# Half-row sums and gate chunks redistributed over a transformer block's mixer, its ring narrowed from six chunks to four, a tenth pair buffer added

## The chip, the core and the metric

The kernel runs on one core of a Trainium2 chip. The metric is the device time of one launch, in microseconds. All data is fp32 and comes from HBM, 556 MB in one launch.

## What is computed

One layer of a hybrid backbone on 256 latent and 256 context tokens of width 2048, cut to its skeleton:

```python
mod = silu(c) @ w_mod + b_mod                  # 6 vectors of 2048: shift, scale, gate (mixer), shift, scale, gate (ffn)
n   = rmsnorm(h, g) * (1 + scale) + shift      # also for the context tokens
z   = n @ w_in                                 # 3584 columns: q 1024, k 256, v 256, gMLP u 512, v 512, conv a 512, g 512
out = concat(window_attention(q, k, v, k_c, v_c, sink), chunk_gmlp(u, v), conformer_conv(a, g)) @ w_out
h   = h + gate_mix * out
m   = rmsnorm(h, g_ffn) * (1 + scale_ffn) + shift_ffn
for e in range(16):                            # top-2 of 16 experts, chosen inside one of 4 groups
    h = h + gate_ffn * combine[:, e] * (silu(m @ w_gate[e]) * (m @ w_up[e])) @ w_down[e]
```

## The kernel before

**Stages.** A schedule written out by hand (`make_schedule`, SCHEDULE) gives the order of TensorE's work. After the modulation vectors and the groups A, G and Q0 of the input projection come the groups KV, Q1, V and U (16 `win` steps each, one for each 128 rows), with single steps of other work between them: `gate` (the gate of the feed-forward, 16 chunks of w_mod), `qT`, `kT`, `convsum`, `convsq`, and three parts for each of eight attention heads (0: scores, 1: transposes of the probabilities, 2: product with V). Then comes the output projection, four groups (`wout`, g) of four chunks; behind the last step of group g VectorE adds the gated residual (L1526 to L1529) and TensorE transposes the sum (`hT`, L766). The router follows, then the jobs: each expert's rows in blocks of up to 96, 16 jobs here. Job 0 is always expert 15, whose loads need no router.

**The ring.** `ring` has eight slots of 1 MB. Six of them (PRE_SLOTS) take the chunks of the mixer in turn, in the order of CHUNK_STEPS (95 chunks; `place`, L378). SyncE waits until TensorE has used the chunk six places earlier (`slot_free`, L425) and issues the next (L438). The other two slots are four half slots of 512 KB.

**Half-row sums.** Three of the six modulation vectors, 6 halves of 1024 columns in all, are computed on VectorE: `sum_rows(n)` (L1303 to L1313) takes the next n of 96 rows, waits for each row's load (`half_in`) and for the sum before (`half_step`), and adds row times silu(c) to an accumulator (L1311). GpSimd loads row m into half slot m % 4 as soon as sum m - 4 is done (`load_rows`, L494 to L498), in order. There are two accumulators; `start_half(i)` (L487 to L492) clears one and loads its bias once TensorE has read the half two before it. TensorE reads half i in a step ("half", i) (L587 for i of 2 and more), which needs the first 16(i+1) sums. Halves 0 and 1 are read behind the scores of heads 4 and 7; halves 2 to 5 behind (`wout`, 0, 3), (1, 3), (2, 2) and (3, 1). VectorE's sums stand at fixed places of its own order: 2 ahead of Q0's norm, 5 and 3 ahead of head 0, then between the two softmax steps of each head and behind it, then 17, 16, 13 and 7 ahead of the four residual adds of the projection.

**Pairs.** A job has 12 loads of 2 MB (four each of gate, up and down weights). `job_pairs` names nine buffers of 2 MB: four are pairs of ring slots, the others lie over tensors of the mixer that are dead by then. `first_pairs` gives job 0's buffers in the order of use, `next_pairs` those of the later jobs, which turn over six buffers. SyncE issues job 0's loads behind the last chunk of the mixer, in an order of its own (L441 to L460), each behind the wait that frees its buffer; the loop of the later jobs stands behind them (L462 to L469) and releases by `last_use`.

**Job 0 on the other engines.** TensorE computes gate and up products (L932 or L937), then `table()` for the later jobs, then the down product (L956 or L962). ScalarE copies the residual into `total` (L1230) once pair 6 has been used, and then copies the transposed hidden rows (L1234), for which the down product waits.

Of the kernel before, what the change touches and what calls it, by code (L numbers as in the profile page):

```python
# [9 lines left out]
ALU = mybir.AluOpType  # L10
# [3 lines left out]
P = 128  # L14
D = 2048
# [37 lines left out]
def make_schedule():  # L53
# [28 lines left out]
    halves = {4: 0, 7: 1}  # L82
    hpos = 0
    for g in range(KV_, 7):
        for c in range(4):
# [50 lines left out]

def constants():
# [22 lines left out]
        "slots_n": one * (np.arange(P) % BASE)[None],  # L160
        "slots_m": one * (np.arange(P) % REST)[None],
        "slots_w": one * (REST + np.arange(P) % BASE)[None],
        "slots_0": one * (BLK + np.arange(P) % REST)[None],
# [11 lines left out]
        "cos": cosd, "sin": sind,  # L175
    }
# [17 lines left out]
CONST_COLS = CONST_AT["cos"][0]  # L194
FIRST_CONSTS = CONST_AT["before"][0]


def build(nc, x, ctx, params, consts, b_half, b_gate, w_mix0, w_mix, w_half, w_gmod, w_in, w_out, w_gate, w_up, w_down, out):
    with ExitStack() as stack:
# [19 lines left out]
        silu_c = sb("silu_c", [P, KT, 32])  # L219
        modcol = sb("modcol", [P, 5, KT, 2])  # L220
# [3 lines left out]
        wr_scaled = sb("wr_scaled", [P, KT, NE])  # L224
# [15 lines left out]

        def k_(name):
            at, n = CONST_AT[name]
            if at >= CONST_COLS:
                return heads[:, at - CONST_COLS:at - CONST_COLS + n]
            return const[:, at:at + n]
# [128 lines left out]
        first_kind = sem("first_kind")  # L374
# [3 lines left out]
        def place(n):  # L378
            return (n - NPRE) % PRE_SLOTS

        def slot(n):
            return ring[:, place(n), :]
# [36 lines left out]
        def _(sp):  # L419
            sp.dma_start(param[:, 0:FIRST_PARAMS], params[:, 0:FIRST_PARAMS]).then_inc(par_in, 16)  # L420
            sp.dma_start(const[:, 0:FIRST_CONSTS], consts[:, 0:FIRST_CONSTS]).then_inc(const_in, 16)
            for t in range(TT):
                sp.dma_start(tokens[:, t, :], x[t * P:(t + 1) * P, :]).then_inc(x_in[t], 16)
            for n, (kind, *at) in enumerate(CHUNK_STEPS):
                sp.wait_ge(slot_free, n + 1)  # L425
# [12 lines left out]
                sp.dma_start(to, src).then_inc(landed[place(n)], 16)  # L438
                if n == NUMBER["win", Q0_, 12]:
                    sp.dma_start(const[:, FIRST_CONSTS:], consts[:, FIRST_CONSTS:CONST_COLS]).then_inc(table_in, 16)  # L440
            weights = (w_gate, w_up, w_down)  # L441
# [1382 lines left out]
```

## Time and profile before

| | us |
|---|---|
| median of 3 runs | 1443.22 (1439.74 to 1447.37) |
| profiled execution, whole | 1449.17 |
| its span | 1447.4 |
| TensorE matmul busy | 1299.3 (90%) |
| VectorE busy | 423.1 (29%) |
| ScalarE busy | 209.1 (14%) |
| DMA read | 556 MB, 386 GB/s over the span |

The profile is of one execution. In its views PE is TensorE's matmuls, PEld its weight loads, DVE VectorE, ACT ScalarE, POOL GpSimd, SP SyncE; `x16` counts instructions, a bracket such as `[4.75 <-DVE big L1529]` is the idle time ahead of an instruction and the line that ended it. q1 is the queue of SyncE's loads, q0 that of GpSimd's (the half rows). The granted clock is TensorE's, as a share of 2.4 GHz. A view by stage has for each stretch its length, then busy us and instruction count of PE, PEld, DVE, ACT and POOL, then the granted clock, the DMA engines' busy share and GB/s.

### The profile page before, as it was taken

What the parts mean: (1) busy time and instruction counts of PE and PEld (TensorE: products, weight loads), DVE (VectorE), ACT (ScalarE), POOL (GpSimd) and SP (SyncE); (2) the same over time, 40 slices, a digit from 0 to 9 for tenths busy, and PEclk for the clock granted to TensorE, in tenths of its full rate; (3) what the DMA queues carried; (4) which work ended last, traced back from release to release, by engine and by line L of the source; (5) the groups of instructions that cost most, each with busy time, mean ns of one, the idle gap of its engine ahead of it and who ended that gap; (6) DMA issues with size and microseconds to landing.
All of it is one profiled execution on the core that took longest, in us unless ns stands there. A gap on an engine that the chain in (4) does not pass through costs nothing.

```text
span 1447.4 us, 20580 instructions
## 1 busy us (share of the span) xinstructions
PE 1299.3 (90%) x8742; PEld 618.0 (43%) x8743; DVE 423.1 (29%) x803; ACT 209.1 (14%) x488; POOL 73.6 (5%) x138
## 2 busy tenths in 40 slices
PE   6899999999989998999999999997887887878857
PEld 4556444545445465433632543442442442333223
DVE  2002885877666340202111201021110111111112
ACT  2002101343001133100200110110110110011001
POOL 0001301121322000000000000000000000000000
PEclk9999999999999899999999999999999999999988
DMA  9999659687998899999999999999999999999996
GB/s 380 409 420 384 252 233 397 217 279 271 346 377 313 334 368 426 427 426 424 427 427 415 418 428 427 411 428 427 429 427 428 427 430 428 429 429 428 427 428 263
DMA packets 57450, 559.56 MB, mean 387 GB/s; under 512 B 6688, under 2 KB 6816, under 8 KB 20768
## 3 DMA queue, kind: packets, MB, share of 16 engines
q1 hardware_dynamic: 42768, 504.35, 83.4%
q0 software_dynamic: 14320, 52.01, 9.9%
q10 hardware_dynamic: 288, 2.10, 0.3%
q8 instruction: 60, 0.98, 0.3%
q14 instruction: 14, 0.11, 0.0%
HBM read 556.34 MB, written 2.10 MB: 386 GB/s over the span
## 4 chain that ended last, share of the span: by engine, by line
PE 52%; DMA 39%; DVE 5%; issue 2%; ACT 1%; DVEq 0%; SPq 0%; ACTq 0%
DMA ring<-w_up_dram 11%; PE ps L932 9%; DMA ring<-w_gate_dram 9%; PE ps L937 8%; PE ps L640 7%; DMA ring<-w_half_dram 6%; PE ps L899 5%; PE ps L956 4%; DMA ring<-w_down_dram 4%; DMA big<-w_up_dram 4%; PE ps L962 3%; DVE once L1311 3%; DMA ring<-w_in_dram 3%; PE ps L634 2%; PE ps L645 2%
## 5 line engine op out<-in xcount | busy, mean ns | idle before, releaser
L1680 DVE TENSOR_TENSOR big<-ps,big 128x1024 f32<-128x1024 f32 x60 | 70.7, 1220 | 306.5 <-PE ps L885 161.0
L937 PE MATMUL ps<-ring,big 128*64 128x512 f32 x560 | 132.9, 608 | 22.1 <-DMA ring<-w_up_dram 10.6
L640 PE MATMUL ps<-ring,big 128*128 128x512 f32 x320 | 148.1, 602 | 2.9 <-DMA ring<-w_in_dram 2.3
L1311 DVE SCALAR_TENSOR_TENSOR once<-ring,silu_c,once 128x1024 f32<-128x1024 f32 x96 | 123.2, 1283 | 62.9 <-DMA ring<-w_half_dram 57.2
L899 PEld LDWEIGHTS ps<-probs,big 128*128 128x128 f32 x1024 | 119.2, 191 | 44.3 <-issue 37.6
L899 PE MATMUL ps<-probs,big 128*128 128x96 f32 x1024 | 129.8, 280 | 1.9 <-DVE probs L1684 1.9
L932 PE MATMUL ps<-ring,early 128*32 128x256 f32 x1408 | 90.4, 406 | 30.8 <-DMA ring<-w_up_dram 18.3
L753 PE MATMUL ps<-ring,big 128*128 128x512 f32 x240 | 109.5, 614 | 0.0
L640 PEld LDWEIGHTS ps<-ring,big 128*128 128x128 f32 x320 | 58.4, 191 | 70.4 <-issue 64.8
L937 PEld LDWEIGHTS ps<-ring,big 128*64 128x64 f32 x560 | 36.2, 137 | 104.6 <-issue 66.9
L962 PE MATMUL ps<-ring,once 128*64 128x512 f32 x336 | 77.5, 598 | 3.4 <-DMA ring<-w_down_dram 3.4
L932 PEld LDWEIGHTS ps<-ring,early 128*32 128x32 f32 x1408 | 44.3, 115 | 76.9 <-DMA ring<-w_up_dram 22.6
L956 PE MATMUL ps<-ring,once 128*32 128x512 f32 x576 | 73.2, 602 | 0.3 <-DMA ring<-w_down_dram 0.3
L753 PEld LDWEIGHTS ps<-ring,big 128*128 128x128 f32 x240 | 46.9, 198 | 56.9 <-issue 56.9
L1216 ACT ACTIVATE big<-ps,modcol,scale_ffn 128x96 f32<-128x96 f32 x112 | 39.1, 429 | 206.1 <-PE ps L899 206.1
L1712 DVE TENSOR_TENSOR once<-ps,early 128x512 f32<-128x512 f32 x12 | 8.3, 692 | 192.3 <-PE ps L956 125.4
L498 POOL DMA_DIRECT2D ring<-w_half_dram x96 | 51.1, 532 | 256.9 <-DVE once L1311 256.9
L1216 ACT ACTIVATE early<-ps,modcol,scale_ffn 128x96 f32<-128x96 f32 x144 | 50.3, 429 | 77.7 <-PE ps L899 77.7
L634 PE MATMUL ps<-big,ring 128*128 128x256 f32 x256 | 58.5, 382 | 1.6 <-DMA ring<-w_in_dram 1.6
L937 PE MATMUL ps<-big 128*64 128x512 f32 x224 | 52.4, 600 | 7.5 <-DMA big<-w_up_dram 5.0
L634 PEld LDWEIGHTS ps<-big,ring 128*128 128x128 f32 x256 | 47.8, 190 | 12.5 <-DMA ring<-w_in_dram 4.7
L932 PE MATMUL ps<-big,early 128*32 128x256 f32 x608 | 40.4, 414 | 13.9 <-DMA big<-w_up_dram 7.9
(320 smaller groups left out, 1094.0 us busy)
## 6 DMA issues: line engine op xcount, KB each, us to landing
ring<-w_down_dram SPq DMA_DIRECT2D x48, 2048.0 KB, 23.4
ring<-w_up_dram SPq DMA_DIRECT2D x46, 2048.0 KB, 23.0
ring<-w_gate_dram SPq DMA_DIRECT2D x33, 2048.0 KB, 22.1
ring<-w_half_dram POOLq DMA_DIRECT2D x96, 512.0 KB, 5.9
big<-w_up_dram SPq DMA_DIRECT2D x18, 2048.0 KB, 22.3
ring<-w_mix_dram SPq DMA_DIRECT2D x32, 1024.0 KB, 11.0
late<-w_down_dram SPq DMA_DIRECT2D x16, 2048.0 KB, 23.7
big<-w_gate_dram SPq DMA_DIRECT2D x15, 2048.0 KB, 25.4
```

What stands on the lines that cost most here:

```text
L498: pool.dma_start(half_slots[:, m % HALF_SLOTS, :], w_half[m]).then_inc(half_in[m % HALF_SLOTS], 16)
L634: mm = pe.matmul(Z[b + q // 2][:, (q % 2) * SEQ:(q % 2 + 1) * SEQ], w[:, q * P:(q + 1) * P], nT[:, k, 0:SEQ], start=(k == 0 and q % 2 == 0 ...
L640: mm = pe.matmul(ps[:, b + t, :], nT[:, k, t * P:(t + 1) * P], w, start=(k == 0), stop=(k == KT - 1))
L753: mm = pe.matmul(ps[:, b + t, :], mixT[:, k, t * P:(t + 1) * P], w[:, i, :], start=(k == 0), stop=(k == KT - 1))
L899: mm = pe.matmul(Yb[:, i, at:at + BLK], tokens[:, t, k * P:(k + 1) * P], one_hot[:, t, :], start=(t == 0), stop=(t == TT - 1))
L932: mm = pe.matmul(out_b[0][BASE * f:BASE * (f + 1), :], rows[0][:, k, :], w[:, kk, f * 256:(f + 1) * 256], start=(k == 0), stop=(k == KT - 1))
L937: mm = pe.matmul(out_b[1][REST * f:REST * (f + 1), :], rows[1][:, k, :], w[:, kk, f * N:(f + 1) * N], start=(k == 0), stop=(k == KT - 1))
L956: mm = pe.matmul(Db[0][BASE * q:BASE * (q + 1), :], hT[0][:, (i % 2) * P + BASE * (i // 2):(i % 2) * P + BASE * (i // 2 + 1)], w[:, q * N: ...
L962: mm = pe.matmul(Db[1][REST * (q // 2):REST * (q // 2 + 1), q % 2, :], hT[1][:, (i % 4) * P + REST * (i // 4):(i % 4) * P + REST * (i // 4 ...
L1216: last = act.activation(to[:, k, :], Yb[:, k // 4, at:at + BLK], ACT.Identity, bias=modcol[:, 3, k, 0:1], scale=scale_ffn[:, k:k + 1])
L1311: stt(total, half_slots[:, m % HALF_SLOTS, :], silu_c[:, m % KT, 0:1], total, ALU.mult, ALU.add) \
L1680: tt(y, Yb[:, 2 * h:2 * h + 2, :].rearrange("p a n -> p (a n)"), y, ALU.add).then_inc(summed, 1)
```

## The change

- **Gate chunks:** two behind each quarter of KV and of Q1, instead of three in KV and two behind the first halves of Q1.
- **Sums:** 4 behind the convolution, 3 behind the key rotation, 4 and 3 around the start of the conv variance (before: 5 and 3 there), so that 16 instead of 10 stand ahead of head 0; 15, 15, 12 and 5 in the projection instead of 17, 16, 13 and 7. The gate's bias add moves behind head 1. Halves 0 and 1 are read behind heads 3 and 6.
- **Ring:** from V's first chunk on (NARROW) the mixer uses four slots instead of six. PLACE, EARLIER and LANDINGS hold each chunk's slot, the chunk that had it before, and the count of landings.
- **Pairs:** a tenth buffer, `extra`. Job 0's first load goes into it, ahead of the chunks of Q1; its sixth goes into ring slots 4 and 5 (pair 3) once all of Q1 is used. Pair 6 waits for 88 sums. `first_pairs` and `next_pairs` follow; the tables of slot numbers are loaded last, into `silu_c`, and GpSimd's descriptor scratch shrinks to 4096 bytes to make room.
- **Table:** `table()` of job 0 stands behind its fifth half load instead of behind its eighth.

```diff
@@ make_schedule
-    halves = {4: 0, 7: 1}
+    halves = {3: 0, 6: 1}
-            if g == KV_:
-                seq += [("gate", 3 * c + i) for i in range(3)]
-            elif g == Q1_ and c < 2:
-                seq += [("gate", 12 + 2 * c + i) for i in range(2)]
+            if g in (KV_, Q1_):
+                seq += [("gate", 2 * c + i + (8 if g == Q1_ else 0)) for i in range(2)]
@@
+NARROW, NARROW_SLOTS = NUMBER["win", V_, 0], 4
+PLACE = [(n - NPRE) % (PRE_SLOTS if n < NARROW else NARROW_SLOTS) for n in range(NPRE)]
+EARLIER = [max((m for m in range(n) if PLACE[m] == PLACE[n]), default=n - PRE_SLOTS) for n in range(NPRE)]
+LANDINGS = [PLACE[:n + 1].count(PLACE[n]) for n in range(NPRE)]
@@ build
+        extra = sb("extra", [P, 2 * CH])
-        wr_scaled = sb("wr_scaled", [P, KT, NE])
+        job_slots = silu_c[:].rearrange("p k n -> p (k n)")
+        wr_scaled = late[:, 0:KT * NE].rearrange("p (k e) -> p k e", k=KT)
-        job_pairs += [nT_all[:, 0:2 * CH], big[:, TT * D:2 * TT * D], once[:]]
+        job_pairs += [nT_all[:, 0:2 * CH], big[:, TT * D:2 * TT * D], once[:], extra[:]]
-        first_pairs = (0, 1, 8, 2, 3, 6, 7, 4, 5, 0, 1, 2)
-        next_pairs = (3, 4, 5, 0, 1, 2, 3, 4, 5, 0, 1, 2)
+        first_pairs = (9, 0, 1, 8, 2, 3, 6, 7, 4, 5, 0, 1)
+        next_pairs = (2, 3, 4, 5, 0, 1, 2, 3, 4, 5, 0, 1)
@@ sync
-                sp.wait_ge(slot_free, n + 1)
+                if n == NARROW + NARROW_SLOTS:
+                    sp.wait_ge(slot_free, used_chunk(NARROW - 1))
+                    sp.dma_start(job_pairs[3], weights[5 // 4][FIRST_EXPERT, 5 % 4]).then_inc(job_landed[3], 16)
+                if n == NUMBER["win", Q1_, 0]:
+                    sp.dma_start(job_pairs[first_pairs[0]], weights[0][FIRST_EXPERT, 0]) \
+                        .then_inc(job_landed[first_pairs[0]], 16)
+                sp.wait_ge(slot_free, used_chunk(EARLIER[n]))
-            for i in (5, 2, 0, 1, 3, 4, 6, 7, 8, 9, 10, 11):
+            for i in (6, 3, 1, 2, 4, 7, 8, 9, 10, 11):
                 if s == 6:
                     sp.wait_ge(slot_free, used(U_))
+                    sp.wait_ge(half_step, HALF_SLOTS + 6 * KT - 8)
-                elif i < 9:
-                    sp.wait_ge(slot_free, used_job(2 * s + 1 - SLOTS))
+                elif i < 10:
+                    sp.wait_ge(slot_free, used_job(2 * s - 1 - NARROW_SLOTS) if s else used_chunk(NARROW - 1))
@@ gpsimd, behind the last half row
+            pool.wait_ge(half_step, HALF_SLOTS + 6 * KT)
+            pool.dma_start(job_slots[:], consts[:, LAST_COLS:ALL_COLS]).then_inc(slots_in, 16)
@@ tensor, experts
-                    if m == 1 and first:
-                        table()
-                    elif m == 1:
+                    if m == 1 and not first:
...
+                        if first and m == 0 and i == 4:
+                            table()
@@ vector
             ts(small[:, 32:33], small[:, 63:64], 1.0, None, ALU.mult).then_inc(conv_done, 1)
+            sum_rows(4)
...
             finish_heads(N)
 
+            sum_rows(3)
             dve.wait_ge(csum_done, 1)
...
-            sum_rows(5)
-            dve.wait_ge(gate_bias_in, 16)
-            dve.wait_ge(slot_free, used_chunk(NUMBER["gate", KT - 1]))
-            tt(modrow[:, 1, :], M, modrow[:, 1, :], ALU.add).then_inc(gate_saved, 1)
+            sum_rows(4)
...
                 if h == 1:
+                    dve.wait_ge(gate_bias_in, 16)
+                    dve.wait_ge(slot_free, used_chunk(NUMBER["gate", KT - 1]))
+                    tt(modrow[:, 1, :], M, modrow[:, 1, :], ALU.add).then_inc(gate_saved, 1)
                     head_norm(2)
...
-                sum_rows((17, 16, 13, 7)[g])
+                sum_rows((15, 15, 12, 5)[g])
@@ kernel
-    nc = bacc.Bacc("TRN2", target_bir_lowering=False, num_devices=1)
+    nc = bacc.Bacc("TRN2", target_bir_lowering=False, num_devices=1, dynamic_dma_scratch_size=4096)
```

## Rows read from the trace of the kernel before

**Rows 1.** The page's slices, DMA busy share in tenths of 40 equal slices.
```profile
DMA  9999659687998899999999999999999999999996
```

**Rows 2.** Busy time by stage; then granted clock, DMA share, GB/s.
```profile
198.00:216.00 18.00, 18.00 (x61) 7.14 (x59) 14.99 (x39) 0.00 (x0) 0.00 (x0) 1.00 0.58 234
216.00:257.00 41.00, 41.00 (x159) 19.14 (x159) 24.59 (x46) 8.12 (x15) 4.23 (x8) 1.00 0.95 383
...
360.00:478.00 118.00, 111.70 (x319) 54.54 (x317) 76.67 (x64) 11.04 (x27) 30.28 (x55) 0.97 0.90 335
...
540.00:968.00 428.00, 412.95 (x3686) 180.37 (x3678) 62.23 (x111) 58.50 (x164) 0.00 (x0) 1.00 1.00 423
968.00:1430.00 462.00, 370.76 (x2720) 162.51 (x2720) 66.95 (x118) 45.45 (x124) 0.00 (x0) 0.96 1.00 427
```

**Rows 3.** TensorE's waits, 540 to 968 us: total us, times, longest.
```profile
PE ps L932 <- DMA ring<-w_gate_dram: 1.0, 1, 1.0
```

**Rows 4.** The job loop's loads (L469) issued 903 to 922 us.
```profile
DMA to landing us min/median/max: 8.6/9.2/10.1
```

**Rows 5.** TensorE's waits, 120 to 540 us.
```profile
PE ps L699 <- DVE probs L1454: 3.1, 3, 2.2
```

**Rows 6.** TensorE in order of time, heads and projection: start us, us, what.
```profile
320.68 3.48 PE L640 MATMUL ps<-ring,big 128*128 128x512 f32 x4
...
359.78 7.03 PE L753 MATMUL ps<-ring,big 128*128 128x512 f32 x16
...
390.77 1.84 PE L587 MATMUL ps<-const,once 128*128 128x1 f32 x16
...
434.46 1.97 PE L766 MATMUL ps<-const,big 128*128 128x128 f32 x8 [4.75 <-DVE big L1529]
...
476.96 2.81 PE L587 MATMUL ps<-const,once 128*128 128x1 f32 x16 [1.55 <-DVE once L1311]
479.63 9.61 PE L753 MATMUL ps<-ring,big 128*128 128x512 f32 x16
```

**Rows 7.** TensorE in order of time, end of KV and head 0.
```profile
216.35 2.78 PE L596 MATMUL ps<-ring,silu_c 128*32 128x512 f32 x24
...
255.47 1.04 PE L699 MATMUL ps<-const,probs 128*128 128x128 f32 x8
```

**Rows 8.** VectorE in order of time, convolution to head 0.
```profile
165.24 47.60 DVE L1412 SCALAR_TENSOR_TENSOR once<-yT,late,once 128x256 f32<-128x256 f32 x120
...
217.51 1.22 DVE L1367 TENSOR_REDUCE ss<-work 128x8 f32<-128x1024 f32 x1 [4.48 <-ACT work L1109]
...
231.62 5.46 DVE L1311 SCALAR_TENSOR_TENSOR once<-ring,silu_c,once 128x1024 f32<-128x1024 f32 x4
...
247.59 1.28 DVE L1311 SCALAR_TENSOR_TENSOR once<-ring,silu_c,once 128x1024 f32<-128x1024 f32 x1 [4.29 <-DMA ring<-w_half_dram]
...
250.51 1.23 DVE L1445 TENSOR_REDUCE small<-ps 128x2 f32<-128x1024 f32 x1 [1.30 <-PE ps L688]
```

**Rows 9.** DMA queues, 240 to 254 us: packets, MB, share.
```profile
q1 hardware_dynamic: 528, 3.93, 67.0%
q0 software_dynamic: 519, 1.89, 33.4%
```

**Rows 10.** Half-row loads (L498) issued at 234.6 us, then at 237.4 us.
```profile
DMA to landing us min/median/max: 5.5/5.5/5.5
...
DMA to landing us min/median/max: 10.2/10.2/10.2
```

**Rows 11.** VectorE in order of time, projection group 1.
```profile
408.63 4.06 DVE L1311 SCALAR_TENSOR_TENSOR once<-ring,silu_c,once 128x1024 f32<-128x1024 f32 x3 [5.36 <-DMA ring<-w_half_dram]
...
431.87 1.28 DVE L1526 TENSOR_TENSOR work<-ps,early 128x512 f32<-128x512 f32 x2
```

**Rows 12.** ScalarE in order of time, job 0.
```profile
534.11 3.70 ACT L1230 COPY big<-big 128x2048 f32<-128x2048 f32 x2
```

**Rows 13.** TensorE in order of time, start of job 0.
```profile
522.10 3.66 PE L932 MATMUL ps<-ring,early 128*32 128x256 f32 x64
```

More of the change, by code:

```diff
@@ L159, in constants @@
         "slots": one * np.arange(BLK)[None],
[L160 to L163, printed above, removed]
         "jobno": one * np.arange(JOBS)[None],
@@ L175, in constants @@
         "cos": cosd, "sin": sind,
+        "slots_n": one * (np.arange(P) % BASE)[None],
+        "slots_m": one * (np.arange(P) % REST)[None],
+        "slots_w": one * (REST + np.arange(P) % BASE)[None],
+        "slots_0": one * (BLK + np.arange(P) % REST)[None],
     }
@@ L194 @@
 CONST_COLS = CONST_AT["cos"][0]
+LAST_COLS = CONST_AT["slots_n"][0]
 FIRST_CONSTS = CONST_AT["before"][0]
@@ L239, in build @@
         heads = rope_heads[:, 1024:2048]
+        job_slots = silu_c[:].rearrange("p k n -> p (k n)")
+        wr_scaled = late[:, 0:KT * NE].rearrange("p (k e) -> p k e", k=KT)
         def k_(name):
             at, n = CONST_AT[name]
+            if at >= LAST_COLS:
+                return job_slots[:, at - LAST_COLS:at - LAST_COLS + n]
             if at >= CONST_COLS:
@@ L373, in build @@
         dve_step, spread_saved = sem("dve_step"), sem("spread_saved")
-        first_kind = sem("first_kind")
+        first_kind, slots_in = sem("first_kind"), sem("slots_in")
         block = stack.enter_context(nc.Block())
-        def place(n):
-            return (n - NPRE) % PRE_SLOTS
         def slot(n):
-            return ring[:, place(n), :]
+            return ring[:, PLACE[n], :]
         def used_chunk(n):
@@ L437, in _ @@
                     src = w_gmod[at[0]]
-                sp.dma_start(to, src).then_inc(landed[place(n)], 16)
+                sp.dma_start(to, src).then_inc(landed[PLACE[n]], 16)
                 if n == NUMBER["win", Q0_, 12]:
                     sp.dma_start(const[:, FIRST_CONSTS:], consts[:, FIRST_CONSTS:CONST_COLS]).then_inc(table_in, 16)
-            weights = (w_gate, w_up, w_down)
-            for i in (5, 2, 0, 1, 3, 4, 6, 7, 8, 9, 10, 11):
+            for i in (6, 3, 1, 2, 4, 7, 8, 9, 10, 11):
                 s = first_pairs[i]
@@ L483, in _ @@
             pool.wait_ge(scaled, 2 * TT)
-            pool.dma_start(heads[:, 0:ALL_COLS - CONST_COLS], consts[:, CONST_COLS:ALL_COLS]).then_inc(misc_in, 16)
+            pool.dma_start(heads[:, 0:LAST_COLS - CONST_COLS], consts[:, CONST_COLS:LAST_COLS]).then_inc(misc_in, 16)
             pool.dma_start(param[:, FIRST_PARAMS:PARAMS], params[:, FIRST_PARAMS:PARAMS]).then_inc(rest_in, 16)
@@ L523, in _ @@
                 if n is not None:
-                    pe.wait_ge(landed[place(n)], 16 * len(range(n, -1, -PRE_SLOTS)))
+                    pe.wait_ge(landed[PLACE[n]], 16 * LANDINGS[n])
                 if kind == "mod":
@@ L1157, in _ @@
                     act.activation(bufA[:], ps[:, 0:2, :], ACT.Gelu_apprx_tanh).then_inc(gelu_v, 1)
-                if h in (4, 7):
-                    save_half(h // 7)
+                if h in (3, 6):
+                    save_half(h // 6)
                 save_pT(h)
@@ L1508, in _ @@
                     link(stt(scale_ffn[:], modcol[:, 4, :, 0], 1.0, ffn_g, ALU.add, ALU.mult))
-                    tt(wr_scaled[:], wr, scale_ffn[:].unsqueeze(2).broadcast_to([P, KT, NE]), ALU.mult) \
+                    tt(wr_scaled, wr, scale_ffn[:].unsqueeze(2).broadcast_to([P, KT, NE]), ALU.mult) \
                         .then_inc(wr_ready, 1)
@@ L1666, in _ @@
             dve.wait_ge(table_ready, 1)
+            dve.wait_ge(slots_in, 16)
             dve.wait_ge(slot_free, used_job(2 * first_pairs.index(8) + 1))
```

1 line of the change is left out of this document (added).

## The prediction

> **What bounds the kernel now.** I read the page's slices first, then busy times by stage, TensorE's waits, and the order of time at the two places that the change touches. The slices show the DMA full at both ends and partly empty between about 145 and 360 us [rows 1]. By stage it moved 234 GB/s at the end of group KV, 383 in Q1 with a share of 0.95, 335 in the output projection, 423 and 427 in the jobs [rows 2]. It is tempting to read 900 us at 425 GB/s as "DMA-bound, so whatever is loaded earlier is won". That is only half right. From 540 to 968 us TensorE is busy 413 of 428 us and waited for a DMA once, for 1.0 us [rows 2, 3]. The 2 MB loads of the job loop took 8.6 to 10.1 us from issue to landing at 903 to 922 us [rows 4], with 4.9 us of pure transfer (2.097 MB at 427 GB/s): hardly one load was queued ahead. The DMA there leads by as much as TensorE's release of buffers allows, so after 968 us, where TensorE is busy only 371 of 462 us, the DMA starts from a position that TensorE set. What shifts job 0 on TensorE shifts the end; a lead of the DMA alone is lost by 920 us.
>
> So the sum is made on TensorE's path to job 0, whose start is at 522.1 us. Up to the projection it waits three times for softmax rows, 3.1 us together [rows 5]. In the projection it waits 4.75 us for a residual add and 1.55 us for the last half-row sum, and after such waits its clock is for a while at 1.2 instead of 2.4 GHz: the chunk at 479.63 took 9.61 us against 7.03 at 359.78, and four matmuls at 320.68 took 3.48 against 1.88 [rows 6].
>
> **Gate chunks spread.** KV loses four gate chunks, Q1 gains four. Three of them take 2.78 us [rows 7], 0.92 each: TensorE reaches Q1 3.6 us earlier (219.1 less 3.6 is 215.5 us) and does the four there; no work is saved. For the DMA it matters: Q1 now wants three 1 MB chunks every 9 us throughout, KV three in 16 us instead of four.
>
> **Pair 9, in KV.** It is issued behind the load of gate 7, for which gate 3 must be used: about 183 us. Transfer 4.9 us, into a stretch at 234 GB/s in which the next chunk can't be asked for before 198 us. Cost nothing; without that cover, 4.9 us.
>
> **Sums before head 0.** This is the expensive edit. Before, VectorE did 8 half-row sums between 231.6 us and head 0; now it does 14 (4 behind the convolution, 3 behind the key rotation, 4 and 3 around the conv variance). The first four have their rows in the ring and start at 213 us: at 1.37 us each (5.46 for four) they end at 218.5 and delay the key norm, 217.51 before, by 1.0 us, which TensorE doesn't see until its key transposes at 235 us [rows 8]. The other ten need fresh 512 KB loads, the first issued at 214.4 us. From 214.8 on, nine chunks for Q1 and three for V follow each other on the SP queue without a break. With both queues full, 240 to 254 us, q1 completed 528 packets and q0 519: one for one [rows 9]. A chunk and a half-row load are 128 packets each, so 1047 packets in 14 us is 3.74 us for a pair of them and the ten loads take 37.4 us. A load into a freer DMA needed 5.5 us [rows 10], 1.3 of it transfer, and I split the rest into 2.8 before the data and about 2 behind: row 15 lands at 217.2 + 37.4 + 2 = 256.6 us and its sum ends at 257.9. Then the variance, and head 0's maximum at 258.4 instead of 250.51; TensorE's transposes of the probabilities came 4.96 us behind that [rows 7, 8], so 263.3. TensorE would be there at 253.9 (255.47, less two gate chunks that now come behind it, and its overlap). **Stall: 9.4 us**, and queued behind it are the rest of Q1, V and U. Bounds: at the pace of the projection, where q1 is lightly loaded (1.94 us a sum, below), ten loads would be in at 241 us and the stall 0; if the first contended load is as late as the one that landed 10.2 us after its issue [rows 10], 11.5. I take 9.4, since the packet counts are of this very stretch. Behind so long a wait comes a low-clock spell, 0 to 2.6 us; I take 1.6, as at 320.68.
>
> The Trainium skill, "DMA: Bandwidth & Descriptors", Queues, rings and completion order, says that a DMA engine goes round robin between the queue rows it has work for, a packet at a time. The counts of 528 and 519 agree. By that rule a half row's 4 KB packet takes turns with a chunk's 8 KB one however urgent it is, which speaks against these sums under Q1's chunks.
>
> **Heads, ring of four, pair 3.** The sums for each head are as many as before, so the 3.1 us of waits stay. With four slots a chunk is issued at least 28 us ahead of its use. No cost, at most 2 us. Pair 3 goes out when gate 15 is used, near 268 us, when four half rows are in stock. Nothing. The gate bias add behind head 1 lies beside TensorE's work. Nothing.
>
> **Projection.** 47 sums stand here instead of 53, as 15, 15, 12 and 5. Let t be the time since the first output chunk began (359.78 before). Half 2 is read at t = 31.0 to 32.8 [rows 6], and row 64 can't be loaded before, as there are two accumulators: memset and bias load take 2 us, the row 5.6, t = 40.4. Twelve sums from 408.63 to 431.87 us are 1.94 each [rows 11]; fifteen end at t = 69.5, the residual add at 72.0; TensorE asks at 69.9 (434.46 less 4.75). So it waits 2.1 instead of 4.75 us (saves 2.65), with a spell of 1.6 instead of about 2.9 (saves 1.3; 1.97 against 1.04 on the transposes, the rest on the chunk). Bounds: wait 0 to 4.75. Twelve sums more end at t = 95, the last five, four of them in stock, between 107 and 111, where TensorE asks at 111: the wait of 1.55 goes, with 0.97 on half 5 (2.81 against 1.84) and 2.58 on the chunk behind it [rows 6]. Pair 6 now waits for 88 sums and no longer delays rows 86 to 89. **Saved: 2.65 + 1.3 + 1.55 + 0.97 + 2.58 = 9.0 us**; bounds 4 and 12.7. What is late next is the projection's own 16 chunks of 7 us.
>
> **Job 0.** ScalarE's two copies of the residual, 3.70 us from 534.11 [rows 12], wait for 1.8 us more of job 0, and ScalarE's next copy, 1.2 us of slack behind them, releases the down projection: +0.6. The table comes earlier; pairs 8, 0, 1, 2, 7, 4 and 5 each land 8 us or more ahead of their use. The descriptor scratch is smaller; a queue with at most four half rows shows no limit, I take 0, bounds 0 to 5.
>
> **Sum.** 9.4 + 1.6 - 9.0 + 0.6 = +2.6 us on the profiled execution: span 1447.4 to 1450.0, with the 1.8 us around it 1451.8 against 1449.2. That execution is 6 us above the median of the runs, 1443.2, and the difference goes on the median: 1445.8 us. Half a percent, 7.2 us, is about what a measurement of this kernel can tell from no change.
>
> **Rivals.** First, **no stall at head 0**: rows 6 to 15 land in time, because chunks pause or q0 gets more than its turn. For it: three loads landed 5.5 us after issue; against it the packet counts. 1445.8 - 11.0 = 1434.8 us. Second, **the buffers pay**: 4.2 MB, 9.8 us of transfer, is in before the projection ends, and the tenth pair is a lead of 4.9 us into the jobs. Before, three reloads stand behind the first chunks of job 0, now two, issued 1.8 us later: a lead of about 3 us. If the jobs used it, beside no stall, 1431.5; a full pair, 1430. Against it: rows 3 and 4. Third, the slow side, **the projection gives nothing back**: row 64 gated by half 2 and row 80 by half 3 leave VectorE as late at the second add as now (74.7), and pair 6 meets the last five sums. It decides once fifteen sums take over 31 us from t = 40.4 instead of 29. Then 9.4 + 1.6 + 0.6 less at most 3 is +9 to +12: 1452 to 1455 us.
>
> **Numbers.** Forecast (1440 to 1450) 0.47; no stall 0.25; buffers pay 0.09; nothing given back 0.19. Below 1436.0: over half of the second case, the third, a little of the first: 0.28. Above 1450.4: most of the last case, a little of the first: 0.20. The range runs from the third case to the top of the last, 1431 to 1455.
>
> **What would show it.** A wait of TensorE for VectorE's probabilities of about 9 us near 254 us, VectorE waiting for half rows between 227 and 257 us; the wait at the second residual add down to 2 us and none at half 5; the first output chunk 11 us later, job 0 within 4 us of 522 us [rows 13]; landing times near 900 us as short as now. It is wrong if head 0's maximum starts by 252 us, or if the end moves by more than the start of job 0 does.

## The result, and the profile after

The changed kernel takes 1455.46 us (median of nine runs, 1449.99 to 1457.97), 1.0063 times the kernel before (95% interval 1.0044 to 1.0082): **9.1 us slower** (6 to 12). Forecast was +2.6 us, to 1445.8. The kernel before, timed beside it nine times, has a median of 1445.3 us without one run of 3280 us, 2.1 above the 1443.22 of three runs from which the forecast counted. The profiled execution of the changed kernel took 1456.65 us, its span 1454.8 against 1447.4.

Where the time went shows in four steps through the profile after. In the page's slices TensorE's busy row has a dip in the eighth, 255 to 291 us, where the heads start; the DMA's row is as full in the jobs as in [rows 1]:

```profile
PE   6899999798999998999999999997888887878866
DMA  9999669776899889999999999999999999999996
```

The table by stage, columns as in [rows 2], each stretch moved with its stage:

```profile
198.00:216.00 18.00, 18.00 (x63) 7.02 (x65) 17.86 (x44) 0.93 (x2) 0.44 (x1) 1.00 0.45 175
216.00:264.00 48.00, 39.43 (x152) 17.40 (x140) 27.82 (x46) 6.28 (x13) 8.46 (x16) 0.95 1.01 412
374.00:492.00 118.00, 115.02 (x335) 56.10 (x334) 70.30 (x61) 11.11 (x28) 26.25 (x48) 0.99 0.90 342
540.00:975.00 435.00, 418.29 (x3775) 183.54 (x3764) 64.75 (x120) 62.59 (x167) 0.00 (x0) 1.00 1.00 420
975.00:1440.00 465.00, 376.92 (x2738) 164.51 (x2741) 66.36 (x116) 46.96 (x128) 0.00 (x0) 0.95 1.00 424
```

Q1 and head 0 (second row) now have TensorE idle for 8.6 of 48 us; the jobs (last two) are what they were. TensorE's waits from 120 to 545 us (total us, times, longest), to be held against [rows 5, 6]:

```profile
PE ps L717 <- DVE probs L1471: 13.1, 4, 8.7
PE ps L784 <- DVE big L1549: 1.5, 1, 1.5
PE ps L605 <- DVE once L1329: 1.4, 1, 1.4
```

In TensorE's order of time (start us, us, what, wait ahead of it), head 0, then the second residual add and half 5, as in [rows 6, 7], then job 0, as in [rows 13]:

```profile
264.14 1.97 PE L717 MATMUL ps<-const,probs 128*128 128x128 f32 x8 [8.71 <-DVE probs L1471]
265.90 3.62 PE L658 MATMUL ps<-ring,big 128*128 128x512 f32 x4
...
445.89 1.09 PE L784 MATMUL ps<-const,big 128*128 128x128 f32 x8 [1.53 <-DVE big L1549]
...
485.42 1.95 PE L605 MATMUL ps<-const,once 128*128 128x1 f32 x16 [1.44 <-DVE once L1329]
487.23 8.81 PE L771 MATMUL ps<-ring,big 128*128 128x512 f32 x16
...
528.95 1.93 PE L948 MATMUL ps<-extra,early 128*32 128x256 f32 x32
```

Job 0 starts 6.85 us later than before and the span is 7.4 us longer: the loss is complete before the jobs begin. The rest from the last transposes of the projection to the end of the span (L784 at 506.80 us; before, L766 at 500.00) is 948.0 us, before 947.4.

### The profile page after: what moved, and what is told of

Same layout as the page of the kernel before. It is cut to its first block, busy times and chain, and to the rows that moved or that the text cites. A ratio compares the mean times of both kernels' runs of the same rounds, so it can differ in the third digit from the quotient of the medians.

```text
span 1454.8 us, 20582 instructions
## 1 busy us (share of the span) xinstructions
PE 1302.0 (89%) x8742; PEld 618.3 (43%) x8743; DVE 422.7 (29%) x803; ACT 209.3 (14%) x488; POOL 73.8 (5%) x139
## 3 DMA queue, kind: packets, MB, share of 16 engines
q1 hardware_dynamic: 42768, 504.09, 83.2%
## 4 chain that ended last, share of the span: by engine, by line
PE 49%; DMA 37%; DVE 9%; issue 2%; ACT 2%; DVEq 0%; SPq 0%; POOL 0%; ACTq 0%
DMA ring<-w_up_dram 14%; PE ps L948 9%; DMA ring<-w_gate_dram 9%; PE ps L953 9%; DMA ring<-w_half_dram 8%; PE ps L917 5%; PE ps L974 5%; PE ps L980 4%; DVE once L1430 3%; DMA ring<-w_mix_dram 3%; PE ps L658 3%; DVE once L1329 3%; PE ps L771 2%; PE ps L652 2%; DMA ring<-w_down_dram 2%
## 5 line engine op out<-in xcount | busy, mean ns | idle before, releaser
L953 PE MATMUL ps<-ring,big 128*64 128x512 f32 x672 | 158.7, 606 | 23.2 <-DMA ring<-w_up_dram 15.6
L948 PE MATMUL ps<-ring,early 128*32 128x256 f32 x1664 | 109.5, 414 | 40.3 <-DMA ring<-w_up_dram 25.4
L953 PEld LDWEIGHTS ps<-ring,big 128*64 128x64 f32 x672 | 43.6, 137 | 121.3 <-issue 82.1
L948 PEld LDWEIGHTS ps<-ring,early 128*32 128x32 f32 x1664 | 53.7, 117 | 96.9 <-DMA ring<-w_up_dram 32.6
L980 PE MATMUL ps<-ring,once 128*64 128x512 f32 x224 | 51.9, 598 | 2.3 <-DMA ring<-w_down_dram 2.3
L1252 ACT COPY once<-ps 128x256 f32<-128x256 f32 (+1 forms) x19 | 8.3, 452 | 306.8 <-PE ps L968 306.8
L974 PE MATMUL ps<-ring,once 128*32 128x512 f32 x384 | 47.6, 600 | 1.2 <-DMA ring<-w_down_dram 1.2
L1430 DVE SCALAR_TENSOR_TENSOR once<-yT,late,once 128x256 f32<-128x256 f32 x120 | 47.6, 483 | 0.0
```

The costliest lines, as they stand in the source:

```text
L948: mm = pe.matmul(out_b[0][BASE * f:BASE * (f + 1), :], rows[0][:, k, :], w[:, kk, f * 256:(f + 1) * 256], start=(k == 0), stop=(k == KT - 1))
L953: mm = pe.matmul(out_b[1][REST * f:REST * (f + 1), :], rows[1][:, k, :], w[:, kk, f * N:(f + 1) * N], start=(k == 0), stop=(k == KT - 1))
L974: mm = pe.matmul(Db[0][BASE * q:BASE * (q + 1), :], hT[0][:, (i % 2) * P + BASE * (i // 2):(i % 2) * P + BASE * (i // 2 + 1)], w[:, q * N: ...
L980: mm = pe.matmul(Db[1][REST * (q // 2):REST * (q // 2 + 1), q % 2, :], hT[1][:, (i % 4) * P + REST * (i // 4):(i % 4) * P + REST * (i // 4 ...
L1430: ins = stt(acc[:, q, :], yT[:, q, tap:tap + SEQ], conv_cols[:, q, tap:tap + 1], acc[:, q, :], ALU.mult, ALU.add)
```

## The experiments

Each kernel was timed beside the kernel before. Ratios are turned into us at 1446, and an interval of a ratio is some 2 to 3 us to either side. "Head 0", "2nd add" and "half 5" are TensorE's waits there in the one profiled execution; "projection" is its length from the first chunk to the last transposes; "pair 6" is the time from that first chunk to the issue of pair 6 on SyncE's queue.

| kernel | ratio (95%) | us | head 0 | 2nd add | half 5 | projection | pair 6 |
|---|---|---|---|---|---|---|---|
| before | | 0 | 0 | 4.75 | 1.55 | 140.2 | 85.9 |
| before, again | not timed | | 0 | 2.40 | 2.34 | 137.0 | 80.7 |
| after | 1.0063 (1.0044, 1.0082) | +9.1 | 8.71 | 1.53 | 1.44 | 132.4 | 95.4 |
| after, again | not timed | | 8.92 | 3.28 | 2.85 | 135.5 | 97.2 |
| e2: sums alone | 1.0011 (0.9993, 1.0029) | +1.6 | 6.35 | 2.27 | 0 | 131.4 | 82.2 |
| e3: gates alone | 0.9998 (0.9985, 1.0012) | -0.3 | 0 | 0 | 2.09 | 131.3 | 78.1 |
| e4: ring and pairs alone | 1.0033 (1.0013, 1.0054) | +4.8 | 0 | 3.76 | 5.30 | 141.8 | 99.3 |
| e10: e4, pair 6 free | 1.0028 (1.0010, 1.0047) | +4.0 | 0 | 3.20 | 5.82 | 142.4 | 98.4 |
| e16: narrow pace alone | 1.0034 (1.0015, 1.0053) | +4.9 | 0 | 0 | 4.54 | 136.5 | 93.7 |
| e1: after, 13 sums | 0.9998 (0.9981, 1.0015) | -0.3 | 0 | 0 | 3.59 | 135.4 | 93.7 |
| e9: after, chunks in two | 0.9983 (0.9968, 0.9999) | -2.5 | 0 | 3.22 | 1.48 | 137.5 | 98.8 |
| e6: after, pair 6 last | 1.0037 (1.0019, 1.0054) | +5.4 | 9.64 | 2.82 | 0 | 130.3 | 108.7 |
| e5: before, pair 6 last | 0.9984 (0.9965, 1.0004) | -2.3 | 0 | 0 | 0 | 127.2 | 106.9 |
| e8: e1, pair 6 last | 0.9960 (0.9945, 0.9974) | -5.8 | 0 | 3.75 | 0 | 132.9 | 110.7 |
| e11: e8 without ring and pairs | 0.9951 (0.9932, 0.9971) | -7.1 | 0 | 0.98 | 0 | 128.4 | 104.6 |
| e15: e10, chunks and pair 6 split | 1.0055 (1.0035, 1.0074) | +8.0 | 0 | 1.48 | 5.42 | 139.1 | 95.8 |
| e12: e11, chunks in two | 0.9957 (0.9942, 0.9972) | -6.2 | 0 | 3.70 | 0 | 133.9 | 109.3 |

### The wait at head 0: is it the sums, and is it the packets?

**e1** takes out the last three sums ahead of head 0 (the expectation names another three; the number is the same) and **e2** makes the redistribution of sums alone:

```diff
 e1, on the changed kernel
-                sum_rows(3)
                 dve.wait_ge(centred, 1)
...
-                sum_rows((15, 15, 12, 5)[g])
+                sum_rows((17, 15, 13, 5)[g])
```

> The changed kernel, but 13 instead of 16 half-row sums stand ahead of head 0: the three behind the key rotation move into the projection (17, 15, 13, 5). Everything else, the ring of four, the tenth pair, the gates, is as in the changed kernel. Theory A (the time is lost because ten half-row loads run under Q1's chunks at 3.75 us each, and VectorE has to sum them all before head 0): seven such loads are done about 11 us earlier, so TensorE waits at head 0 under 1 us instead of 8.7; no low-clock spell behind it; first output chunk at 360 to 363 us instead of 374.4; the second residual add waits about as before; job 0 starts at 513 to 518 us instead of 529.0; time 6 to 10 us below the kernel before. Rival B (the ring of four, the early pair or the gates shift the mixer whatever the sums do): first output chunk stays beyond 370 us, time at or above the kernel before.

> The kernel before with only the sums redistributed: 4 behind the convolution, 3 and 4 and 4 up to head 0, 15, 15, 12 and 5 in the projection, halves 0 and 1 read behind heads 3 and 6. Gates, ring of six and nine pairs stay. Theory A: ten half-row loads still run beside about ten chunks of Q1 and V, so a wait of TensorE for VectorE's probabilities of 7 to 9 us at head 0, a spell behind it, projection 7 to 8 us shorter, job 0 at 523 to 527 us, time 1 to 4 us above the kernel before. Rival C (with four gates in KV, Q1's chunks leave gaps enough): a wait under 3 us, time 5 us or more below the kernel before.

> The kernel before with only the gate chunks spread (two behind each quarter of KV and Q1) and the gate's bias add behind head 1. Ten half-row sums stand ahead of head 0, as before. Theory A: SyncE's chunks now follow each other without a break under the half rows, so six of them arrive at 3.75 us each; the last one lands near 253 instead of about 247 us, TensorE waits 2 to 6 us at head 0, and the projection is as before: job 0 2 to 6 us later, time 2 to 8 us above the kernel before. Rival D (only the number of sums ahead of head 0 counts): wait at head 0 under 1 us, time within 1.5 us of the kernel before.

With thirteen sums the wait at head 0 is gone and 9.4 us with it (1.0063 to 0.9998): rival B falls. But the time is that of the kernel before, not 6 to 10 us below it. Part of that is half 5, which waits 3.59 us (below) and which the expectation left out. Job 0 does start at 515.86 us, inside the expected range; but that range was counted from the profiled execution of the kernel before, 1449.17 us, which is 4 us above the median of 1445.25 beside e1. With the sums alone the wait is there, with gates and ring as before, and half 5 waits for nothing. TensorE in e2:

```profile
263.29 1.97 PE L699 MATMUL ps<-const,probs 128*128 128x128 f32 x8 [6.35 <-DVE probs L1456]
265.05 3.62 PE L640 MATMUL ps<-ring,big 128*128 128x512 f32 x4
...
479.10 1.84 PE L587 MATMUL ps<-const,once 128*128 128x1 f32 x16
480.81 7.11 PE L753 MATMUL ps<-ring,big 128*128 128x512 f32 x16
```

Rival C falls. The wait is shorter than the 7 to 9 us of theory A and job 0 starts at 519.48 us, earlier than expected; the time, +1.6 us, is in theory A's range, with zero in its interval. With the gates alone there is no wait at head 0 and no measurable difference, as rival D had it. There my arithmetic was wrong: the last of six contended loads was summed at 246.39 us, 4.7 us ahead of head 0's maximum. Spreading the gates costs something only where ten loads have to be in: waits of 8.71, 8.92 and 9.64 us (after twice, e6) instead of the 6.35 us of e2's one execution.

That the packets take turns is what the counts say. After, 232 to 246 us (queue, packets, MB, share), as in [rows 9]:

```profile
q1 hardware_dynamic: 534, 3.97, 68.0%
q0 software_dynamic: 524, 1.90, 33.9%
```

and VectorE's sums in that stretch come at one pace, 3.75 us, each ended by a half-row load:

```profile
242.90 1.29 DVE L1329 SCALAR_TENSOR_TENSOR once<-ring,silu_c,once 128x1024 f32<-128x1024 f32 x1 [2.48 <-DMA ring<-w_half_dram]
246.63 1.28 DVE L1329 SCALAR_TENSOR_TENSOR once<-ring,silu_c,once 128x1024 f32<-128x1024 f32 x1 [2.45 <-DMA ring<-w_half_dram]
250.38 1.28 DVE L1329 SCALAR_TENSOR_TENSOR once<-ring,silu_c,once 128x1024 f32<-128x1024 f32 x1 [2.46 <-DMA ring<-w_half_dram]
...
257.91 1.28 DVE L1329 SCALAR_TENSOR_TENSOR once<-ring,silu_c,once 128x1024 f32<-128x1024 f32 x1 [2.46 <-DMA ring<-w_half_dram]
...
259.44 1.22 DVE L1462 TENSOR_REDUCE small<-ps 128x2 f32<-128x1024 f32 x1
```

**e9** halves the size of SyncE's packets there, and with it doubles the number of its loads. It is the changed kernel, and every chunk from Q1's first to V's last, the gates among them, goes out as two loads of half the width (the counts of landings follow):

```diff
...
-                sp.dma_start(to, src).then_inc(landed[PLACE[n]], 16)
+                if n in IN_TWO:
+                    for i in range(2):
+                        sp.dma_start(to[:, i * (CH // 2):(i + 1) * (CH // 2)], src[:, i * (CH // 2):(i + 1) * (CH // 2)]) \
+                            .then_inc(landed[PLACE[n]], 16)
+                else:
+                    sp.dma_start(to, src).then_inc(landed[PLACE[n]], 16)
```

> The changed kernel with each 1 MB chunk of Q1 and V and the gates between them issued as two loads of half the width, so that SyncE's packets in this stretch are 4 KB like those of the half rows. Theory A (the two queues take turns packet by packet, so the size of the packets sets the shares): a half row beside two 512 KB loads now costs one pair of packets of 4 KB: 2.4 to 2.6 us apart instead of 3.75, row 15 in about 10 us earlier, wait of TensorE at head 0 under 1.5 us instead of 8.7, unless TensorE then waits for chunks; time 5 to 9 us below the changed kernel. Rival (the share is one of bytes or of loads, or SyncE's queue is served first): rows stay 3.75 us apart and the wait at head 0 stays.

The queues of e9, 236 to 250 us, its sums and head 0:

```profile
q1 hardware_dynamic: 805, 2.92, 52.6%
q0 software_dynamic: 799, 2.79, 49.9%
...
240.55 1.28 DVE L1335 SCALAR_TENSOR_TENSOR once<-ring,silu_c,once 128x1024 f32<-128x1024 f32 x1 [1.27 <-DMA ring<-w_half_dram]
243.12 1.28 DVE L1335 SCALAR_TENSOR_TENSOR once<-ring,silu_c,once 128x1024 f32<-128x1024 f32 x1 [1.29 <-DMA ring<-w_half_dram]
245.67 1.28 DVE L1335 SCALAR_TENSOR_TENSOR once<-ring,silu_c,once 128x1024 f32<-128x1024 f32 x1 [1.27 <-DMA ring<-w_half_dram]
...
254.46 1.09 PE L723 MATMUL ps<-const,probs 128*128 128x128 f32 x8
```

Packets still go one for one, 805 to 799, and as both are now of 4 KB the half rows have half of the bytes: 2.56 us apart, no wait at head 0, and 11.6 us off the changed kernel (1.0063 to 0.9983), more than the 5 to 9 I expected. Order and bytes of SyncE's loads are those of the changed kernel; their number is doubled. A share by bytes, or SyncE's queue served first, would have left the rows 3.75 us apart, so it is the taking of turns by number of packets, the same for both queues, that makes the rows late, and the wait with its clock spell is worth 9 to 12 us (prediction: 11.0). The Trainium skill, "DMA: Bandwidth & Descriptors", Queues, rings and completion order, says that a DMA engine changes between queue rows a packet at a time, and that its packets typically hold several descriptors. Both pairs of counts agree with such turns. But a load of one queue has as many packets here as a load of the other, so the counts can't tell turns of one row from turns of several rows.

### Ring and pairs alone: slower, which I had costed at nothing

**e4** is the changed kernel with sums, halves and gates put back. **e10** is e4 with pair 6 freed of its wait for 88 sums. **e16** is the kernel before with one line more, which gives its six slots the pace of four:

```diff
 e16, on the kernel before
                 sp.wait_ge(slot_free, n + 1)
+                if n >= NUMBER["win", V_, 0] + 4:
+                    sp.wait_ge(slot_free, used_chunk(n - 4))
```

> The changed kernel with the sums, the halves and the gate chunks put back as before: the ring of four from V on, the tenth pair in KV, pair 3 in V, the earlier table and the smaller descriptor scratch are all that is left of the change. Theory A (a lead of the DMA is lost by 920 us): no wait at head 0, projection up to 2 us shorter since pair 6 waits for 88 sums, job 0 within 2 us of 522, time 0 to 3 us below the kernel before. Rival E (the buffers pay: 4.9 to 9.8 us of transfer is in ahead of the jobs): the end moves by 5 us or more against the start of job 0, time 7 to 12 us below. Rival F (the narrow ring or the smaller scratch costs): time above the kernel before by 2 us or more, with waits for chunks of w_in or w_out.

> The kernel with only the ring of four, the tenth pair, pair 3, table and scratch, now with pair 6 issued as in the kernel before (behind the last chunk, without the wait for 88 sums). Theory G (the 4.7 us that this part cost come from pair 6 issued at sum 88, whose packets meet the last half rows): the gap in the sums is back at 450 to 460 us, wait at half 5 down from 5.3 to 2.5 us or less, time within 1.5 us of the kernel before. Rival F (ring of four, early pair or pair 3 cost it): still 3 to 6 us above the kernel before.

> The kernel before with one wait more: from V's fifth chunk on SyncE issues a chunk only when the one four places earlier is used (ring of six slots, nine pairs and all else as before). Theory N (the narrow ring is what costs in the kernels with only ring and pairs: the output projection's last chunks, and pair 6 queued behind them, go out 14 to 18 us later and meet the last half rows): pair 6 issued at 458 to 462 us instead of 443 to 446, wait at half 5 of 4 to 6 us instead of 1.6 to 2.3, time 2.5 to 6 us above the kernel before. Rival P (the early loads of pair 9 and pair 3 cost it): wait at half 5 as before, time within 1.5 us of the kernel before.

e4 is 4.8 us slower, against theory A and rival E. Rival F has the time but not its sign: TensorE's one wait for a chunk of w_in is 0.8 us. e10, which should have given the time back, did not (+4.0, and 5.82 us of wait at half 5): theory G, which blamed the wait for 88 sums, falls in that form. e16 has no early load at all, and costs the same 4.9 us (its pair 6 goes out at 453.5 us, earlier than I expected, and the wait is there all the same): it is the narrow ring (theory N), and pairs 9 and 3 need no share in it, within the intervals. How, is on SyncE's queue. Its issues in the kernel before, the changed kernel and e16 (start us, us over which the group stretches, line, what):

```profile
429.75 15.89 SPq L438 DMA_DIRECT2D ring<-w_out_dram  x2
445.68 0.43 SPq L460 DMA_DIRECT2D big<-w_up_dram  x1
```

```profile
428.86 40.86 SPq L453 DMA_DIRECT2D ring<-w_out_dram  x6
469.85 0.36 SPq L475 DMA_DIRECT2D big<-w_up_dram  x1
```

```profile
429.89 23.59 SPq L440 DMA_DIRECT2D ring<-w_out_dram  x4
453.53 0.42 SPq L462 DMA_DIRECT2D big<-w_up_dram  x1
```

Pair 6 (`big<-w_up_dram`) goes out right behind the last chunk of the projection in all three. With four slots that chunk can be asked for only two chunks' work later. Between executions without a wait at the second add, the last chunk is issued 77.7 us after the first output chunk with six slots (e5) and 93.3 with four (e16): 15.6 us. So the last chunks and pair 6 meet the last half rows, which had the DMA to themselves before, and half 5 is late. Of the two it is pair 6 that matters: e6 and e8 below keep the ring of four, only pair 6 goes out later, and half 5 waits for nothing. TensorE in e16:

```profile
472.22 3.57 PE L589 MATMUL ps<-const,once 128*128 128x1 f32 x16 [4.54 <-DVE once L1313]
475.65 9.93 PE L755 MATMUL ps<-ring,big 128*128 128x512 f32 x16
```

4.54 us of wait, 1.73 more on half 5 and 2.8 more on the chunk behind it. The output chunks were never late for TensorE, which is all that the prediction had looked at.

**e15** asks whether packet sizes are behind this too: e10, the projection's chunks in two and pair 6 in four loads.

> The kernel with only ring of four and pairs (pair 6 issued freely), with the chunks of the output projection issued as two loads and pair 6 as four, all of 4 KB packets. Theory A in the projection (turns are taken packet by packet; a half row waits for as many packets of SyncE as it has itself, and these are now 4 KB instead of 8 and 16): the gaps of 4 to 5.5 us in the sums at 449 to 475 us shrink below 3 us, the wait at half 5 falls from 5.8 to under 2 us, time 3 to 6 us below that kernel, so 0 to 2 us around the kernel before. Rival R (in the projection the half rows are limited by the round trip from sum to landing, not by their share): wait at half 5 stays above 4 us, time unchanged.

Theory A falls here: half 5 waits 5.42 us and the time is +8.0, not around zero. The last half rows come 2.2 to 2.6 us apart instead of behind one long gap (5.57 us in e16), and the time is even 4 us above e10's. The profiles don't show where: their spans are 1451.3 and 1451.2 us, and e15's projection is 3.3 us shorter than e10's. That stays open. My reading, argued and not shown: ahead of head 0 a backlog of chunks that nobody needed yet stood in the rows' way, and smaller packets pushed it aside; here pair 6's 4.9 us of transfer is about all there is beside the last rows, and is paid in one gap or in several small ones.

### Taking pair 6 out of the last sums' way

**e6** (on after) and **e5** (on before) let pair 6 wait for all 96 sums; **e8** is e1 with it, **e11** the same sums, halves and gates on the kernel before with its six slots and nine pairs. The edit in e5:

```diff
                 if s == 6:
                     sp.wait_ge(slot_free, used(U_))
+                    sp.wait_ge(half_step, HALF_SLOTS + 6 * KT)
```

> The changed kernel with pair 6 behind all 96 sums instead of 88. Theory G: the gap of 4.9 us in the sums at 477 to 482 us is gone, TensorE's wait at half 5 (1.4 us) and the slow chunk behind it (8.8 us instead of 7.0) with it; the wait at head 0 stays at 8.7 us; time 2 to 4 us below the changed kernel, still 4 to 7 above the kernel before. Rival H (pair 6 comes too late for job 0): a wait for its load in job 0, time as the changed kernel or above.

> The kernel before with one wait more: pair 6 (2 MB, issued at 445.7 us) waits for all 96 half-row sums. Theory G (while its packets are on q1, the half rows of q0 come in at half pace, and this is what makes VectorE late for half 5): the gap of 7.6 us in the sums at 449 to 457 us is gone, TensorE's wait at half 5 falls from 1.6 to under 0.3 us and the low-clock chunk behind it is gone; job 0 3 to 5 us earlier, time 3 to 5 us below the kernel before. Rival H (pair 6 stands then ahead of four other pairs on SyncE's queue at 480 us): job 0 waits 2 us or more for one of its first loads, and the time is the same or up to 5 us above.

> The kernel of thirteen sums ahead of head 0 (ring of four, tenth pair and spread gates as in the changed kernel), with pair 6 behind all 96 sums. Theory A + G (two causes, each with its own term: the wait at head 0, and pair 6's packets under the last half rows): no wait of TensorE at head 0 and none at half 5, projection to its last transpose 127 to 130 us, time 4 to 8 us below the kernel before (ratio 0.9945 to 0.997). Rival: the causes aren't additive, another wait (heads 4 to 7, the second residual add) takes their place, time within 2 us of the kernel before.

> The same sums, halves, gates and place of pair 6 as in the run ahead of this one, but on the kernel before: ring of six throughout, nine pairs, its table and scratch. Theory L (a lead of the DMA is lost in the jobs, so the tenth pair and the narrow ring are worth nothing): the same time as with them, within 2 us. Rival E (buffers pay): 4 us or more above it. Rival F (ring of four, early pair and pair 3 in V cost the mixer): 3 us or more below it.

In the changed kernel VectorE's sums with pair 6 issued at 469.85, then TensorE at half 5 in e6, with pair 6 issued at 477.07:

```profile
476.00 1.28 DVE L1329 SCALAR_TENSOR_TENSOR once<-ring,silu_c,once 128x1024 f32<-128x1024 f32 x1 [0.40 <-DMA ring<-w_half_dram]
482.17 1.28 DVE L1329 SCALAR_TENSOR_TENSOR once<-ring,silu_c,once 128x1024 f32<-128x1024 f32 x1 [4.89 <-DMA ring<-w_half_dram]
```

```profile
479.12 1.84 PE L605 MATMUL ps<-const,once 128*128 128x1 f32 x16
480.82 7.11 PE L771 MATMUL ps<-ring,big 128*128 128x512 f32 x16
```

Gap, wait and slow chunk are gone together, and 3.8 us with them (1.0063 to 1.0037; the intervals overlap, so the traces have to decide). The late pair 6 costs nothing: no kernel with it shows a wait of job 0 for a load (rival H). On the kernel before, where six slots let pair 6 go out at 445.68 us, the same line takes the wait at half 5 away too and gives 2.3 us, less than I expected and with zero in its interval. The profiled executions of e5 and e6 are 6 us below the medians of their kernels (1437.94 and 1444.45 us against 1444.3 and 1450.33), so only the place of the wait is read from them, not its worth. e8 has neither cause and is 5.8 us faster than the kernel before, though a wait of 3.75 us at the second add kept its projection longer than I expected. e11 is 7.1 us faster (1439.07 us against 1446.55), the best measured; with and without the tenth pair the times agree within 1.3 us, as theory L said.

> The best kernel so far (kernel before, thirteen sums ahead of head 0, gates spread, pair 6 behind all sums; 7.5 us below the kernel before) with all chunks from Q1 to the end of the projection issued as two loads of 4 KB packets. Theory A: half rows 2.5 us apart ahead of head 0, the second residual add without a wait, the heads' waits (3.9 us) partly gone; time 1 to 4 us below that kernel, so 8 to 11 us below the kernel before. Rival R (nothing left is limited by the half rows' share): same time within 1.5 us; rival T (SyncE's queue, now with twice the loads, or the chunks' smaller share make TensorE wait for chunks): above it.

e12 is e11 with its chunks in two: -6.2 us, the same as e11 within the intervals. Rival R held: with thirteen sums nothing that these intervals show is left for the rows' share to decide.

### The two profiles again

> The kernel before, unchanged, for a second profile of it. Theory S (the profile that the prediction was made from shows waits that an execution of median length doesn't have): in the projection the wait of TensorE at the second residual add is under 2.5 us instead of 4.75, the projection from its first chunk to its last transpose takes 131 to 137 us instead of 140.2, and the span is 3 to 7 us shorter than 1447.4. Rival: the second profile repeats the first within 1 us in the projection, wait of 4.75 included, and the kernels made from it differ by their edits.

> The changed kernel, unchanged, for a second profile of it. What is by design repeats: wait at head 0 8 to 9.5 us with half rows 3.75 us apart, first output chunk 374 plus or minus 1.5 us, projection 131 to 134 us to its last transpose, a gap of 4 to 5 us in VectorE's sums behind the issue of pair 6. If the projection is here several us away from 132.4, the scatter between executions is of the size of the effects that are to be explained.

The kernel before, second profile, second add and half 5:

```profile
434.37 1.09 PE L766 MATMUL ps<-const,big 128*128 128x128 f32 x8 [2.40 <-DVE big L1529]
...
476.04 2.70 PE L587 MATMUL ps<-const,once 128*128 128x1 f32 x16 [2.34 <-DVE once L1311]
```

The second add waits 2.40 us instead of 4.75; the projection is 3.2 us shorter, but the span is 1448.3, where theory S wanted 3 to 7 us less than 1447.4, since the heads waited 5.8 us. The wait at head 0 repeats in the changed kernel:

```profile
262.83 1.97 PE L717 MATMUL ps<-const,probs 128*128 128x128 f32 x8 [8.92 <-DVE probs L1471]
264.59 2.67 PE L658 MATMUL ps<-ring,big 128*128 128x512 f32 x4
```

The second add does not repeat (3.28 against 1.53), and the first output chunk (368.6 us) and the projection (135.5) are outside the ranges I gave. From before to after the first output chunk is 14.6 us later in the first pair of profiles and 6.6 in the second, the projection 7.8 and 1.5 us shorter, job 0 6.85 and 5.0 us later. Over the seven kernels with the sums of the kernel before in the projection, the wait at the second add was 4.75, 2.40, 0, 3.76, 3.20, 0, 0 and 1.48 us in eight executions, 1.9 on average. Over the five executions with 15, 15, 12 and 5 sums (after twice, e2, e6, e9) it was 1.53, 3.28, 2.27, 2.82 and 3.22, 2.6 on average: nothing here shows that the new places of the sums shorten it. A single execution doesn't price it. What makes it differ I did not settle.

## Why the prediction was wrong

**What bounds the kernel: right.** From the last transposes of the projection to the end it is 943.9 to 949.3 us in all seventeen profiles, with nine pairs or ten. Behind 540 us TensorE waits for no DMA until 975, and the loads issued at 903 to 935 us landed no sooner than in [rows 4]:

```profile
DMA to landing us min/median/max: 9.1/9.9/13.3
```

The kernel before has 8.6/10.1/12.4 in that same stretch.

**Stall at head 0: right in kind and size.** 3.75 us a row (3.74), maximum at 259.44 (258.4), wait 8.71 and 8.92 (9.4). The spell, read from the transposes and the four matmuls behind, which take 1.04 and 1.88 us at full clock, was 2.67 us in the first profile and 1.72 in the second (1.6). Together 11.4 and 10.6 where I had 11.0; e9 and e1 measure 11.6 and 9.4. The 3.74 us was luck in part: 256 of 1047 packets in 14 us would be 3.42. The trace counts 144 packets for a load, not 128 (42768 for SyncE's 297 loads), which gives 3.85.

**Projection: less than 9.0, and from one of my terms only.** It is shorter by 7.8 us in the first pair of profiles and by 1.5 in the second. The 3.95 us that I booked at the second add were the scatter of one execution, not the kernel's: the wait there is no shorter with the new sums (2.6 us on average against 1.9). What I booked at half 5, 5.1 us, did come in e2, with the ring of six. Taking the stall in e2's own profile, 6.35 us and about 2.7 of spell, from its +1.6 us leaves some 7.4 us that six sums fewer in the projection are worth, most of it at half 5.

**Heads, ring of four, pair 3: this step failed.** "No cost, at most 2 us" was worked out from when chunks are needed; it left out what stands behind them on SyncE's queue. e4, e10 and e16 measure 4.0 to 4.9 us.

**Half 5 and pair 6: the same failure from the other end.** "Pair 6 now waits for 88 sums and no longer delays rows 86 to 89" was half a sentence: it delays row 94 instead, 4.89 us of gap. The wait that should go (1.55) was 1.44 and 2.85, and the slow chunk stayed, 8.81 us in both profiles. Of the 5.1 us that I booked, 1.9 came in the first profile and 0.4 in the second. The wait for 88 sums was not what held pair 6: the 88th sum ended near 464.6 us and pair 6 went out at 469.85, right behind the last chunk. The queue held it, as in e10.

**Job 0: about right.** The copies cost 0.4 us more (0.6). The end moved 0.5 us more than job 0's start, which by my own sign would have spoken against the mechanism; it is this term and not the loads. The early table, the scratch and the moved bias add showed nothing.

**The sum, made anew from the runs:** sums alone +1.6; ring of four with its late pair 6 +4.9; the gates under ten loads +2.4 (8.71 less 6.35, single executions). That is 8.9, measured 9.1. Each of the first two is known to 2 or 3 us only, so that they meet so closely is luck. Against my sum of +2.6 it is 4.9 us for the ring, where I had nothing, and some 1.6 us less from the projection (7.4 for 9.0). The rival that I called "the projection gives nothing back" had the right total, +9 to +12, and half of the mechanism: pair 6 did meet the last five sums. Its other half did not happen: the second add stood 71.5 and 73.2 us behind the first output chunk, not 74.7, and the projection gave its 7 us, of which the ring, which that rival did not have, took 5.

## What to carry to other kernels

When a ring gets fewer slots, ask not only whether its chunks still arrive in time, but what is queued behind its last chunk, when that now goes out, and which small loads it meets. Small loads that have a deadline share the DMA by number of packets with whatever stands beside them: keep them out of stretches with a backlog, or make the backlog's packets as small, which paid ahead of head 0 (e9) and not at half 5 (e15). Price a wait that is to be removed from more than one execution.

## What the runs showed of the hardware

A short wait of TensorE can be paid twice, and the second payment doesn't follow from its length alone. Behind a wait of 1.44 us at half 5 the granted clock is 0.79 of 2.4 GHz from 485 to 490 us, some of it at 1.2 GHz (view by stretch of after):

```profile
480.00:485.00 5.00, 3.98 (x10) 1.47 (x8) 2.21 (x2) 0.00 (x0) 0.00 (x0) 1.00 0.48 196
485.00:490.00 5.00, 4.58 (x20) 2.97 (x21) 0.96 (x3) 0.17 (x1) 0.54 (x1) 0.79 0.54 141
490.00:494.00 4.00, 4.00 (x9) 1.78 (x8) 0.00 (x0) 0.00 (x0) 0.00 (x0) 0.84 0.99 422
```

Half 5 and the chunk behind it, 1.84 and 7.11 us without a wait, took 1.8 us more behind waits of 1.44 and 2.85 (after twice) and 2.09 us (e3), 3.5 more behind 1.48 (e9), 1.55 and 2.34 (before twice), and 3.4 to 4.6 more behind 3.59 to 5.82 (e1, e16, e4, e15, e10). At the second add waits of 0.98 to 3.28 us left the transposes at 1.09 us in seven executions, but behind 2.27 (e2) and 3.20 us (e10) they took 1.92 and 1.97. What decides between the two is not shown.
